# A two-layer hybrid decoder trunk on one core: the S5 mixer's work put in another order

## The reference, cut to what matters

```python
    bu = jnp.einsum('bsgh,gph->bsgp', uf.astype(jnp.complex64), b_bar)
    ...
    _, xs = lax.associative_scan(comb, (a, bu), axis=1)
    y = jnp.einsum('bsgp,ghp->bsgh', xs, c).real + d_skip * uf
    g = jax.nn.gelu(y)
    out = g * jax.nn.sigmoid(g @ w_glu + b_glu)
```

## Time and profile before

| what | value |
|---|---|
| median of 3 runs | 1374.37 us (1372.64 to 1374.88) |
| the profiled execution: its time, its span | 1373.18 us, 1371.4 us |
| busy: PE, PE weight load, DVE, ACT, POOL | 1316.9, 1065.1, 849.8, 500.6, 612.7 us |
| the chain that ended last, by engine | PE 80%, DVE 9%, ACT 3%, issue 2%, SP queue 2%, POOL 2% |
| granted TensorE clock, mean | 0.988 of full speed |
| input projection of layer 0, layer 1 (the first unit to the last) | from 8.8 to 232.5 us, from 695.9 to 904.4 us |

### The profile page before, as it was taken

One profiled execution on the slowest core, in us unless ns is written; L12 is line 12 of the kernel. 1 busy time (PEld: TensorE's weight loads), 2 busy tenths in 40 slices (PEclk: granted clock), 3 DMA queues, 4 the chain that ended last, 5 costly groups with the idle time before them and its releaser, 6 DMA issues.

```text
span 1371.4 us, 16028 instructions
## 1 busy us (share of the span) xinstructions
PE 1316.9 (96%) x6234; PEld 1065.1 (78%) x6234; DVE 849.8 (62%) x1149; ACT 500.6 (37%) x752; POOL 612.7 (45%) x288
## 2 busy tenths in 40 slices
PE   7988999999999999999999799989999999999999
PEld 4767777677888888888877687767778888888887
DVE  7847964656788406776237397646577771277731
ACT  5442355555323212322334234555552332122320
POOL 2966533124444444444468474312254444344442
PEclk9999999999999999999999999999999999999999
DMA  6321232013223322323233112311133333223332
GB/s 212 93 62 40 79 94 81 24 39 108 92 93 108 111 87 86 100 92 101 100 100 99 47 48 79 116 36 47 41 113 98 102 109 106 77 92 93 110 111 87
DMA packets 40939, 120.49 MB, mean 88 GB/s; under 512 B 6432, under 2 KB 10656, under 8 KB 40864
## 3 DMA queue, kind: packets, MB, share of 16 engines
q1 hardware_dynamic: 40864, 119.46, 27.3%
HBM read 114.20 MB, written 2.10 MB: 85 GB/s over the span
## 4 chain that ended last, share of the span: by engine, by line
PE 80%; DVE 9%; ACT 3%; issue 2%; SPq 2%; POOL 2%; DMA 1%; DVEq 0%; POOLq 0%; ACTq 0%
PE bank L492 25%; PE bank L505 23%; PE bank L497 23%; SPq L331 1%; PE bank L494 1%; PE bank L727 1%; PE bank L686 1%; POOL wl L353 1%; PE bank L706 1%; DVE bank L1376 1%; PE bank L716 1%; DVE xl L1137 1%; DVE G L1162 1%; ACT wh L863 1%; DMA raw<-in_w_in 1%
## 5 line engine op out<-in xcount | busy, mean ns | idle before, releaser
L353 POOL TENSOR_TENSOR wl<-raw,wh 128x1024 fp32r<-128x1024 f32 (+3 forms) x208 | 501.9, 2414 | 692.8 <-ACT wh L863 437.2
L863 ACT ACTIVATE wh<-raw 128x1024 fp32r<-128x1024 f32 (+3 forms) x208 | 218.6, 1051 | 283.9 <-PE bank L497 229.0
L492 PE MATMUL bank<-xl,wh 128*128 128x512 f32 x1152 | 308.2, 406 | 2.8 <-DVE xl L1137 2.2
L505 PE MATMUL bank<-xh,wl 128*128 128x512 f32 x1152 | 286.4, 390 | 0.0
L497 PE MATMUL bank<-xh,wh 128*128 128x512 f32 x1120 | 276.8, 389 | 0.0
L492 PEld LDWEIGHTS bank<-xl,wh 128*128 128x128 f32 x1152 | 216.7, 190 | 61.8 <-issue 12.9
L505 PEld LDWEIGHTS bank<-xh,wl 128*128 128x128 f32 x1152 | 215.4, 188 | 45.0 <-issue 0.3
L497 PEld LDWEIGHTS bank<-xh,wh 128*128 128x128 f32 x1120 | 210.2, 188 | 44.1
L1180 DVE TENSOR_TENSOR x<-x,bank 128x512 f32<-128x512 f32 x64 | 44.0, 687 | 225.3 <-PE bank L505 225.3
L492 PE MATMUL bank<-ml,wh 128*128 128x512 f32 x512 | 140.3, 402 | 0.0
L505 PE MATMUL bank<-mh,wl 128*128 128x512 f32 x512 | 127.4, 389 | 0.0
(11 more groups left out here) (292 smaller groups left out, 1271.4 us busy)
## 6 DMA issues: line engine op xcount, KB each, us to landing
raw<-in_w_gu SPq DMA_DIRECT2D x88, 512.0 KB, 3.5
raw<-in_w_in SPq DMA_DIRECT2D x52, 512.0 KB, 3.6
raw<-in_w_dn SPq DMA_DIRECT2D x32, 704.0 KB, 4.0
raw<-in_w_oe SPq DMA_DIRECT2D x16, 384.0 KB, 3.0
raw<-in_w_ol SPq DMA_DIRECT2D x16, 256.0 KB, 2.6
x<-in_x SPq DMA_DIRECT2D x8, 256.0 KB, 6.5
raw<-in_w_first SPq DMA_DIRECT2D x4, 512.0 KB, 4.8
out_x<-x SPq DMA_DIRECT2D x8, 256.0 KB, 4.5
```

What stands on the lines that cost most here:

```text
L353: tt(wl[:, p, 0:cols], raw[:, p, 0:cols], wh[:, p, 0:cols].bitcast(F32), ALU.subtract).then_inc(wl_full, 1)
L492: mm(bank[b][:, :], wh[:, p, k * P:(k + 1) * P], lo[:, k, :], start=(k == 0), stop=False)
L505: w = mm(bank[b][:, :], wl[:, p, k * P:(k + 1) * P], hi[:, k, :], start=False, stop=(k == K - 1))
L863: fn(wh[:, p, 0:cols], raw[:, p, 0:cols], ACT.Copy).then_inc(wh_full, 1)
```

## The change

z is projected first (units 0 and 1), u in units 8 and 9. The six transposed groups of `s5_inputs` are spread so that one stands in each half unit, and ACT copies four of them right behind `prep`. Kernels and windows come one unit later, `local` lies in other tiles, and `s5_windows(1)` no longer waits for `states_ready`. The transfers of u are issued beside the weights of units 11 to 14, those of y beside 20, 21, 25 and 26 (before: 5 to 8; 17, 18, 21, 22). The first half's rotation stays in DVE's step 11, its scan and way back move to steps 14 and 15; the second half moves from steps 14 to 17 to steps 16 to 22, cut into pieces: one rotation part each in 17 and 18, one scan each in 19 and 20, `s5_back` in 21, `s5_out` behind unit 22. Both GELUs go to ACT's step 26, the SiLUs of z to steps 3 and 4, the emission of Mamba-2's output to step 23 (from a copy in `v`). Some of these smaller moves are left out below.

```diff
-        local = [sb(f"s5_local{i}", [P, 4, P], at=offsets[n]) for i, n in enumerate(("bmat", "cf"))]
+        local = [sb(f"s5_local{i}", [P, 4, P], at=offsets["mh"] + (MIXC + i) * T * 4) for i in range(2)]
...
-                if s == 5:
-                    sp.wait_ge(unit_out, unit_out_of(l, 1))
-                if 5 <= s <= 8:
-                    i = (s - 5) // 2
-                    for r in range(2 * (s - 5) % 4, 2 * (s - 5) % 4 + 2):
+                if 11 <= s <= 14:
+                    i = (s - 11) // 2
+                    if s % 2:
+                        sp.wait_ge(unit_out, unit_out_of(l, 8 + i))
+                    for r in range(2 * (s - 11) % 4, 2 * (s - 11) % 4 + 2):
...
-                if s in (17, 18, 21, 22):
-                    i = (s - 17) // 4
-                    if s % 4 == 1:
+                if s in (20, 21, 25, 26):
+                    i = (s - 20) // 5
+                    if s % 5 == 0:
                         sp.wait_ge(y_copied, 2 * l + i + 1)
...
@@ GpSimd
-                    if 6 <= s <= 7:
-                        table(l, 0, s - 6)
-                    if 8 <= s <= 11:
-                        for n in ((0,), (1, 2), (3,), (4, 5))[s - 8]:
+                    if 6 <= s <= 8:
+                        state_terms(l, s - 6)
+                    if 9 <= s <= 10:
+                        table(l, 0, s - 9)
+                    if 11 <= s <= 12:
+                        for n in ((3, 4), (5,))[s - 11]:
                             state_terms(l, n)
-                    if s == 11:
-                        s5_imaginary(l, 0)
-                    if 12 <= s <= 13:
-                        table(l, 1, s - 12)
-                    if s == 15:
-                        s5_imaginary(l, 1)
+                    if 13 <= s <= 14:
+                        table(l, 1, s - 13)
+                    if s in (15, 21):
+                        s5_imaginary(l, (s - 15) // 6)
...
@@ TensorE, s5_windows
                 pe.wait_ge(kernels_copied, l + 1)
-                if i:
-                    pe.wait_ge(states_ready, 2 * (l + 1))
@@ TensorE, beside
-                    if 6 <= s <= 8:
-                        s5_inputs(l, 2 * (s - 6) + 1)
+                    if 6 <= s <= 9:
+                        s5_inputs(l, (1, 2, 4, 5)[s - 6])
                     if s == 9:
+                        m2_decays(0)
+                        m2_scores(0)
+                    if s == 10:
                         s5_windows(l, 0)
@@ TensorE, after unit s
-                    if 6 <= s <= 8:
-                        s5_inputs(l, 2 * (s - 6))
+                    if s in (6, 8):
+                        s5_inputs(l, (0, 3)[(s - 6) // 2])
...
-                    if s == 8:
+                    if s == 9:
                         m2_turn(2)
                         m2_turn(3)
-                    if s == 9:
-                        m2_decays(0)
                         pe.wait_ge(xbc_silu, 6 * l + 6)
                         m2_states(0)
                         m2_states(1)
-                        m2_scores(0)
-                    if s == 9:
-                        s5_kernels(l)
                     if s == 10:
                         m2_states(2)
+                        s5_kernels(l)
+                    if s == 11:
                         m2_decays(1)
                         s5_windows(l, 1)
+                        s5_in(l, 0)
...
                     if s == 13:
                         m2_decays(3)
+                    if s == 16:
                         s5_out(l, 0)
-                    if s == 16:
+                        s5_in(l, 1)
                         m2_norm()
-                    if s == 10:
-                        s5_in(l, 0)
-                    if s == 14:
-                        s5_in(l, 1)
...
-                    if s == 17:
+                    if s == 22:
                         s5_out(l, 1)
@@ ScalarE
-                    if s in (11, 15):
-                        s5_copy((s - 11) // 4)
+                    if 7 <= s <= 10:
+                        s5_inputs((1, 2, 4, 5)[s - 7])
+                    if s == 11:
+                        for i in range(2):
+                            s5_weights(local[i][:].rearrange("p a b -> p (a b)"), bank[6][:, :], local_copied)
+                    if s in (15, 21):
+                        s5_copy((s - 15) // 6)
+                    if s in (17, 23):
+                        y_copy((s - 17) // 6)
...
-                    if s in (20, 24):
-                        gelu((s - 20) // 4)
+                    if s == 26:
+                        gelu(0)
+                        gelu(1)
+                        ln_exp_tables()
@@ VectorE
-            def s5_scan(l, j):
+            def s5_rotate(l, j, part):
...
+            def s5_scan(l, j, parts=(0, 1)):
...
-                    scaled(u[:, i, :].rearrange("p (t c) -> p c t", t=CH), i, "p (c t) -> p c t", t=CH)
+                    scaled(z[:, i, :], i)
...
                     if s == 14:
-                        s5_scan(l, 1)
+                        s5_scan(l, 0)
...
                     if s == 15:
-                        s5_back(l, 1)
+                        s5_back(l, 0)
...
+                    if 17 <= s <= 18:
+                        s5_rotate(l, 1, s - 17)
+                    if 19 <= s <= 20:
+                        s5_scan(l, 1, [s - 19])
+                    if s == 21:
+                        s5_back(l, 1)
+                    if s in (21, 25):
+                        s5_finish(l, (s - 21) // 4)
@@ layout
-    order = [w[:, :, s5:z], w[:, :, xbc:dt], w[:, :, z:xbc], w[:, :, sc + 256:sc + 512], w[:, :, sc + 512:s5],
+    order = [w[:, :, z:xbc], w[:, :, xbc:dt], w[:, :, s5:z], w[:, :, sc + 256:sc + 512], w[:, :, sc + 512:s5],
```

More of the change, by code:

```diff
@@ L981, in _ @@
                         fn(xbc[:, s - 3, :], bank[unit_bank(s - 1)][:, :], ACT.Silu).then_inc(xbc_silu, 1)
-                    if s == 7:
+                    if 3 <= s <= 4:
+                        act.wait_ge(unit_out, unit_out_of(l, s - 3))
+                        fn(z[:, s - 3, :], z[:, s - 3, :], ACT.Silu).then_inc(z_silu, 1)
+                    if s == 8:
+                        ln_exp_tables()
                         act.wait_ge(decay_go, nth(decay_go))
@@ L986, in _ @@
                         fn(s16[:, 7, :], s16[:, 5, :], ACT.Exp).then_inc(decay_exp, 1)
[L987 to L991, removed]
+                    if l == 0 and s == 9:
+                        act.wait_ge(lam_go, 1)
+                        fn(lam2[:, :, :], lam2[:, :, :], ACT.Exp).then_inc(lam_exp, 1)
+                    if s == 10:
                         m2_head(0)
@@ L1004, in _ @@
                         rsqrt_mean(z[:, 0, :], 7, 2 * P, m2_rms)
[L1005 removed]
+                    if s == 23:
                         for i in range(2):
[L1007 removed]
+                            emit(MIXD + i, v[:, i, :])
                     if 17 <= s <= 24:
@@ L1012, in _ @@
                         qk_square(s - 16)
[L1013 to L1017, removed]
+                    if s in (6, 8):
+                        s5_inputs((0, 3)[(s - 6) // 2])
+                    if s == 10:
                         s5_weights(kernels[:, :, CH - 1:, :].rearrange("p i a b -> p i (a b)"),
                                    bank[6][:, 0:2 * P].rearrange("p (i a) -> p i a", i=2), kernels_copied)
[L1020 to L1024, removed]
                     if s >= 25:
                         v_copy(s - 25)
-                    if s in (20, 24):
-                        gelu((s - 20) // 4)
+                    if s == 26:
+                        gelu(0)
+                        gelu(1)
+                        ln_exp_tables()
                 def exps(n):
@@ L1348, in lambda_factors @@
                 own(tt(mlam_all[:, :], mlam_all[:, :], pre[:, :, PRE["linit"]].rearrange("p a b -> p (a b)"), SUB))
-            a5, c5, e5 = [t[:, :] for t in (sA, sC, sE)]
-            def s5_scan(l, j):
+            a5, c5, e5 = [t[:, :] for t in (sA, sE, sE)]
+            def s5_rotate(l, j, part):
                 cs, sn = [t[:, :] for t in tab[j]]
[L1355 to L1359, removed]
-                re, im = bank[2][:, :], bank[3][:, :]
-                own(tt(a5, re, cs, MUL))
-                own(tt(c5, im, cs, MUL))
-                dve.wait_ge(dve_own, owned() - 1)
-                own(tt(re, re, sn, MUL))
-                dve.wait_ge(dve_own, owned() - 1)
-                own(tt(im, im, sn, MUL))
-                dve.wait_ge(dve_own, owned() - 1)
-                own(tt(re, c5, re, SUB))
-                dve.wait_ge(dve_own, owned() - 1)
-                own(tt(im, a5, im, ADD))
-                for back, rows in ((1, re), (0, im)):
-                    dve.wait_ge(dve_own, owned() - back)
+                re, im = bank[2][:, :], bank[3][:, :]
+                if part == 0:
+                    dve.wait_ge(tab_full, nth(tab_full))
```

(28 more changed lines are left out.)

24 lines of the change are left out of this document (7 added, 17 removed).

## The result

The changed kernel takes 1351.18 us (median; 1349.46 to 1352.17), the kernel before 1374.11 beside it: a ratio of 0.9841, 95% interval 0.9829 to 0.9853, some 22.9 us less. The prediction was 1352. The profiled execution takes 1352.17 us with a span of 1350.1: 21.3 us less span than before, against a sum of 21.7.

A forecast was written before the change was run, and what follows sets the result against it. PE, busy 96% of the span, was taken as the bound, with only its gaps and clock to win. 31.8 - 1.3 + 1.0 - 9.8 = 21.7 us off 1373.2 gave 1351.5, stated as 1352 on the median's scale; range 1342 to 1362.

The forecast's parts named there:

- The waits that go, and the clock: Units 7 to 11: S5 waits at L551, L562, L574 go, 23.95 us, plus 7.87 us of low clock; 31.8 us won.
- 0.65 us there in layer 0: Wait left at L551 in layer 0 for ACT's first copy of a transposed group, bounds 0 and 1.5; nothing in layer 1.
- DVE in units 12 to 16: New waits of 1.0 us at `m2_apply(1)` and 0.8 at `s5_out(0)` per layer, against 2.3 at `m2_norm`: net -1.3 us.
- Units 17 to 22: DVE's added S5 pieces just fit; 0.5 us of small waits a layer against 2.0 before: +1.0 us.
- The new stall: `qk_mean(7)` behind unit 24 waits 3.2 us for partner rows; with `v_turn(0)` and clock, 9.8 us lost over both layers.
- the fall in both layers, 1353.5: Clock case behind the unit 24 stall: full 2 us lost in each layer, total 1353.5; one layer 1351.5, none 1349.5.
- Costed at nothing: `scaled` changing places, SP's moved u transfers and POOL's C terms, tables and `low`: no cost on PE, bounds 0 and 5 us.
- Hidden stall: Rival: `y_copy` or the partner comes earlier, so the unit 24 stall's 9.8 us stay won: 1342; chance 0.17.
- DVE bound: Rival: DVE bounds units 12 to 16, waits at their bounds, 9 us less won: 1359; chance 0.22.
- Weights: Rival: POOL sets the pace in units 8 to 12, waits for `wl` or `wh`: 1367, at worst 1373; chance 0.07.
- Slower by a low clock: Rival: clock stays low behind the new stall for about 5 units, 2 x 28 = 56 us: 1407; chance 0.04.
- After 1.23 it did not, after 4.29 it did: Whether PE's clock fell behind idle gaps of those us in units 7 to 9, cited for the 3.2 us stall.

The follow-up runs named there:

- the two kernels that hide it: Changed kernel with the second half's y transfers one unit later: 1341.71 us; changed kernel with ACT's second y copy ahead of `prep`: 1342.13 us.

## Why the prediction was right, step by step

The mechanism and the size were right: 21.3 us of span against 21.7, with the largest gain and the largest loss each within 1 us. Some terms were mis-sized, and their errors cancel.

- **The waits that go, and the clock (31.8; 31.1 measured).** L574 and L562 vanished, and with them the low clock. Re-adding the one wait cost 12.7 us and putting the transposes close cost 6.8, each with some 3 to 5 us of low clock. Taken as separate shares these are 19.5 of the 31.1 us; what made the rest no run isolates. The part that was mis-sized is "0.65 us there in layer 0": it was 2.0. I had followed ACT's list, but the convolution's sums came late from DVE. Two casts that took 0.27 and 0.21 us before took 2.33 and 1.96, and one of the two products beside them got shorter again. The convolution of unit 5 ended 2.1 us later than before (65.3 against 63.2), and ACT, whose SiLU stands ahead of the copy, waited for it until 65.31.
- **DVE in units 12 to 16 (-1.3; -3.2).** The places were right, the waits were 1.21 and 1.36 us a layer where I had 1.0 and 0.8, and the 2.3 us at `m2_norm` went as said. The guess that slower operations beside GpSimd give 1.0 us back for `m2_apply(1)` was a little too kind: `m2_mix(3)` still had one of 2.27 us right ahead of it.
- **Units 17 to 22 (+1.0; +2.7).** I left 0.5 us of waits a layer; there were none, and what goes with a wait is more than its idle time. Before, units with a wait of 0.3 to 0.4 us took 0.5 to 0.6 longer.
- **The new stall (-9.8; -9.7).** Idle 3.31 and 3.33 us where 3.2 were worked out. Two things beside it cancel: the low clock cost 1.7 us in layer 0 (8.01 us from `qk_mean(7)` to `v_turn(0)`, 6.35 at full clock; 8.04 in layer 1), not 1.0; and the 0.7 us at `v_turn(0)` weren't there. DVE had `scaled` of unit 24 done at 207.9, and PE, slowed by its clock, came at 208.3. The clock fell in both layers, at 0.72 granted over 6.2 us. The Trainium skill, TensorE: Matmul & The Clock Gate, Part 1, states that the clock follows how busy PE has been just before. Of the cases that I worked out beside that rule this is the fall in both layers, 1353.5, with a price of 1.7 us in the place of 2. That this term came out within 0.1 us and the total within 0.4 is partly luck: the missing 0.7 us at `v_turn(0)` made up for the clock, and the 1.7 us more won in units 17 to 22 for the 1.9 more lost in units 12 to 16.
- **Costed at nothing.** The moved transfers of u, `scaled`'s changed places and POOL's C terms stopped no one: PE has no wait for `wl`, `wh` or `s_chunks` in units 5 to 14.
- **The rivals.** Hidden stall: no, 3.3 us stand in the trace; the two kernels that hide it land at 1341.7 and 1342.1, where the rival had 1342. DVE bound: in part, 5.1 us of waits where it would have 11. Weights: no. Slower by a low clock: it recovered after one unit.

One price was misread. The prediction put the 3.28 us that layer 0 lost in units 8 and 9 behind the one gap of 4.29 us. The same starts, cut up, give 1.6 us lost from 71.56 to 78.08 and 1.7 from 82.35 to 90.64, behind a second gap, which layer 1 has too:

```profile
82.35 0.82 PE L551 MATMUL bank<-cst,s_powered 128*128 128x128 f32 x3 [1.92 <-ACT s_inputs L949]
...
755.05 0.52 PE L551 MATMUL bank<-cst,s_powered 128*128 128x128 f32 x3 [1.94 <-ACT s_inputs L949]
```

In layer 0 the granted clock is 0.66 in 71.5 to 76.5, 1.00 in 76.5 to 82.3 and 0.64 in 82.3 to 87.0; in layer 1 it is 1.00 in 755 to 760. The sum of 3.28 stands, but the clock also fell behind 1.92 us of idle where a longer gap lay 11 us ahead. "After 1.23 it did not, after 4.29 it did" left that out.

The sum gave the whole of L574's wait to the new buffer ("with `local` elsewhere that wait is not there"). That falls short: the buffer alone gives 6.6 us, and the wait goes on, on DVE; it takes the new order too. The new order with the old wait gives 8.8 us. And "4.94 us for eight transfers is seen in every row of its kind" is not quite so: the kernel before has groups of 4.94 to 5.83 us; the two ahead of the stall took 4.94.

## What to carry to other kernels

When work moves, follow each queue in its order to the next consumer: eight small transfers put ahead of two others cost 10 us over the two layers, and one unit later they cost nothing. A wait removed from one engine can come back by way of another that waits for the same producer, so look whether the producer gets earlier or its consumers come later. Add the clock to a wait's price, and look at the waits around it: two of 1.2 and 1.4 us cost no clock, one of 3.3 cost 1.7 us more than itself, and in layer 0 before one of 1.92 behind a longer one cost as much.

## What the runs showed of the hardware

- The granted clock was 1.00 behind single waits of 1.2, 1.4 and 2.0 us; 0.72 over 6.2 us behind 3.3; 0.67 over 5.1 behind 4.1; 0.50 over 5.6 behind 4.0. The 0.72 came in four places, both layers of two kernels. Three waits of 2.0, 0.7 and 1.6 us within 17 us gave 0.83 over 20 us, and in the kernel before a wait of 1.92 us gave 0.64 over 4.7 us where one of 4.29 lay 11 us ahead; with 1.94 us and none so long ahead it stayed at 1.00. A fall behind 3.3 us cost 1.7 us on top of the idle time.
- A 128x128 cast on DVE took 0.21 to 0.27 us before and 1.96 to 2.42 after. All of the long ones, and the long products beside them, ended 0.08 to 0.15 us behind the GpSimd instruction they overlapped; the short ones started within 0.2 us of the gap between two of its instructions. Moving them four steps didn't make them shorter.
- Eight small transfers between buffers held SP's queue for 4.94 us in most places, and for up to 5.83 in the kernel before.
